# Another order of work in the mixers, the attention, the first feed-forward's head and the last norm, and thirteen products of zeros at the start

## What is computed

```python
# first block
xn = rms_norm(h, g_mix_pre); z = xn @ w_in
y_conf = conformer_conv(...)     # 31-tap depthwise convolution, layer norm, silu, 256x256 product
y_att  = forgetting_attention(...)  # 4 heads, causal, cumulated log gates in the logits
y_sc   = short_conv_mixer(...)   # 3 taps
y_pool = multiscale_pool(...)
h = h + rms_norm(concat(y_conf, y_att, y_sc, y_pool) @ w_out, g_mix_post)
h = h + rms_norm(square(relu(hn @ w_up)) @ w_down, g_mlp_post)
h = h + rms_norm((p @ w_ple_proj) * sigmoid(rms_norm(h) @ w_ple_gate), g_ple_post)
# second block, layer 0: latent attention (8 heads) and differential attention (8 maps), then swiglu
# second block, layer 1: recurrent mixer (state space heads and hgrn2), then swiglu, then the last norm
x = x + swiglu(rms_norm(x), w_gate, w_up, w_down)
out = rms_norm(x, norm_final)
```

## Time and profile before

| | us |
|---|---|
| median of 3 runs | 1001.95 (999.59 to 1003.36) |
| profiled execution | 1000.06 |
| its span, first to last instruction | 998.2 |
| mean granted TensorE clock | 0.992 of full |
| TensorE busy | 953.5 |
| VectorE, ScalarE, GpSimd busy | 700.3, 515.8, 87.1 |
| moved by transfers | 164.4 MB, 165 GB/s on average |

### The profile page before, as it was taken

The page is one execution under the profiler, slowest core; times in us unless marked ns, Lnnn a source line. Parts: engine busy times, 40 slices in busy tenths (PEclk is TensorE's granted clock), DMA queues, the critical chain, the costliest instruction groups (busy, mean ns, idle before and its releaser), DMA issues.

```text
span 998.2 us, 13575 instructions
## 1 busy us (share of the span) xinstructions
PE 953.5 (96%) x5540; PEld 835.9 (84%) x5540; DVE 700.3 (70%) x921; ACT 515.8 (52%) x698; POOL 87.1 (9%) x110
## 2 busy tenths in 40 slices
PE   6997999999999899889999999999989889999997
PEld 5996797888888688778988888888988789888886
DVE  4798785666667887886666666667979676666663
ACT  4776754444436646765543434368645355434341
POOL 4353000000000100000000000000132000000000
PEclk9999999999999999989999999999999999999999
DMA  9732365665565354224665656546321356656531
GB/s 320 245 128 92 120 220 194 199 207 183 174 206 175 112 171 143 85 85 125 215 208 173 207 171 209 169 149 211 127 85 49 121 169 211 207 172 208 172 127 43
DMA packets 106190, 164.40 MB, mean 165 GB/s; under 512 B 2816, under 2 KB 82784, under 8 KB 106000
## 3 DMA queue, kind: packets, MB, share of 16 engines
q1 hardware_dynamic: 104688, 158.25, 48.9%
q0 software_dynamic: 1440, 5.28, 1.5%
HBM read 162.47 MB, written 1.05 MB: 164 GB/s over the span
## 4 chain that ended last, share of the span: by engine, by line
PE 69%; DVE 19%; ACT 6%; issue 4%; DMA 2%; POOL 1%; DVEq 0%; POOLq 0%; ACTq 0%
PE ps L379 67%; DVE wl L1739 6%; DVE SC L1841 2%; PE ps L387 2%; ACT wh L1172 2%; DMA raw<-in_w_in 1%; DVE xhl L1744 1%; DVE xf L1748 1%; ACT junk L1160 1%; DVE st L2139 1%; ACT xhl L1178 1%; POOL st L2496 1%; DVE rows L2339 1%; DVE hs L1759 0%; DVE h L1801 0%
## 5 line engine op out<-in xcount | busy, mean ns | idle before, releaser
L1739 DVE TENSOR_TENSOR wl<-raw,wh 128x2048 fp32r<-128x2048 f32 (+2 forms) x150 | 339.6, 2266 | 153.8 <-ACT wh L1172 153.6
L1172 ACT ACTIVATE wh<-raw 128x2048 fp32r<-128x2048 f32 (+2 forms) x150 | 281.9, 1884 | 156.6 <-PE ps L379 142.8
L379 PE MATMUL ps<-xhl,wh 128*128 128x512 f32 (+1 forms) x1248 | 257.9, 354 | 2.5 <-ACT wh L1237 2.5
L379 PEld LDWEIGHTS ps<-xhl,wh 128*128 128x128 f32 x1248 | 202.4, 193 | 29.9 <-issue 3.7
L379 PE MATMUL ps<-wh,xhl 128*128 128x512 f32 (+3 forms) x1000 | 195.2, 339 | 6.0 <-ACT SC L1435 1.8
L379 PEld LDWEIGHTS ps<-wh,xhl 128*128 128x128 f32 x1000 | 155.1, 190 | 25.3 <-ACT xhl L1178 2.6
L379 PEld LDWEIGHTS ps<-xhl,wl 128*128 128x128 f32 x1008 | 135.6, 191 | 7.5
L379 PE MATMUL ps<-xhl,wl 128*128 128x256 f32 x1008 | 140.6, 282 | 0.0
L379 PE MATMUL ps<-wl,xhl 128*128 128x512 f32 (+3 forms) x500 | 105.2, 336 | 0.0
L379 PE MATMUL ps<-wh,fh 128*128 128x512 f32 x304 | 91.0, 392 | 1.8 <-DVE fl L1986 1.5
L379 PE MATMUL ps<-wh,fl 128*128 128x512 f32 x304 | 90.2, 390 | 0.0
(11 more groups left out here) (266 smaller groups left out, 840.8 us busy)
## 6 DMA issues: line engine op xcount, KB each, us to landing
raw<-in_ffn_gate SPq DMA_DIRECT2D x22, 1024.0 KB, 5.3
raw<-in_ffn_up SPq DMA_DIRECT2D x22, 1024.0 KB, 5.4
raw<-in_ffn_down SPq DMA_DIRECT2D x22, 1024.0 KB, 4.9
raw<-in_w_up SPq DMA_DIRECT2D x16, 1024.0 KB, 5.6
raw<-in_w_down SPq DMA_DIRECT2D x16, 1024.0 KB, 4.9
raw<-in_s_w_in SPq DMA_DIRECT2D x14, 1024.0 KB, 5.4
raw<-in_w_in SPq DMA_DIRECT2D x9, 1024.0 KB, 7.1
raw<-in_a_w_in SPq DMA_DIRECT2D x6, 1024.0 KB, 5.1
```

The costliest lines, as they stand in the source:

```text
L379: return e.matmul(o, a, b, start=start, stop=stop, skip_group_check=True)
L1172: e.activation(high_of(i), raw_of(i), ACT.Copy).then_inc(*up("act_high", i))
L1739: e.tensor_tensor(low_of(i), raw_of(i), high_of(i).bitcast(F32), ALU.subtract).then_inc(*up("dve_lo", i))
```

## The change

It reorders steps on all engines, adds 13 products of zeros into an unused result bank at TensorE's start (`warm`), moves four copies (xs, cb) from ScalarE to VectorE and splits the last norm's product between VectorE and ScalarE. No weight slot is added or left out. The diff is cut to the changed lines, each group with the line before it, and indentation is reduced.

```diff
@@ -479,7 +479,7 @@
-def project_end(n, sl, tb, half, order):
+def project_end(n, sl, tb, half, order, x_low=None):
@@ -487,6 +487,8 @@
         for x in (xh, xl):
+            if x is xl and i == order[2] and x_low:
+                e.wait_ge(*x_low)
@@ -513,9 +515,18 @@
 def first_mixer():
+    def warm(n):
+        for i in range(n):
+            mm(ps[7][:, 0:256], upad[:, 0, 0:128], upad[:, 0, 0:256], True, True)
+    e.wait_ge(*at("pool_zero", 2))
+    warm(6)
...
     norm_turn(0, 0)
+    warm(2)
     norm_turn(0, 1)
+    warm(5)
@@ -670,9 +681,9 @@
-    def down_block(j, tb):
+    def down_block(j, tb, halves=(0, 1)):
         x = [y[:, j % 3, :].rearrange("p (k n) -> p k n", k=2) for y in (fh, fl)]
-        tok(down[j], [(ps[ACC[s_next][tb][c]][:, :], HALF[c]) for c in range(2)], tb, 0, j == 0, False, x)
+        tok(down[j], [(ps[ACC[s_next][tb][c]][:, :], HALF[c]) for c in halves], tb, 0, j == 0, False, x)
@@ -725,14 +736,16 @@
         e.wait_ge(*at("dve_head_low", l, 0, 4))
-        down_block(0, 0)
+        down_block(0, 0, (0,))
+        e.wait_ge(*at("dve_head", l, 1, 0))
+        head_turn(1, 0, 4, 7)
+        down_block(0, 0, (1,))
         e.wait_ge(*at("dve_head", l, 1, 1))
-        head_turn(1, 0, 4, 7)
         head_turn(1, 4, 2, 2)
-        e.wait_ge(*at("dve_head_low", l, 1, 4))
-        down_block(0, 1)
...
         head_turn(1, 6, 2, 5)
+        e.wait_ge(*at("dve_head_low", l, 1, 0))
+        down_block(0, 1)
@@ -828,6 +841,8 @@
         if i == 8:
+            e.wait_ge(*at("act_qk_turned", 1, 1, 0))
+        if i == 9:
@@ -894,7 +909,7 @@
         if i == 1:
-            e.wait_ge(*at("act_qk_turned", 1, 0, 0))
+            e.wait_ge(*at("act_qk_turned", 0, 0, 1))
@@ -1010,7 +1025,7 @@
             elif n == 1:
-                e.wait_ge(*at("act_cb", tb))
+                e.wait_ge(*at("dve_cb", tb))
@@ -1025,7 +1040,7 @@
         if n == 0:
-            e.wait_ge(*at("act_xs", 0))
+            e.wait_ge(*at("dve_xs", 0))
@@ -1087,7 +1102,6 @@
     e.wait_ge(*at("act_xbc", 3))
-    feat(S["hq"][1], ps[0])
@@ -1098,6 +1112,7 @@
         mm(o[:, 256:384], xb[:, 4 + g, 128:256], xb[:, 6 + g, 128:256], True, True).then_inc(*up("pe_cb", g))
+    feat(S["hq"][1], ps[0])
@@ -1128,9 +1143,9 @@
     project(6, sl, 0, 1, order, at("dve_mix3_low", 0, 1))
-    e.wait_ge(*at("dve_mix3_low", 1, 0))
+    e.wait_ge(*at("act_part_high", 6, 1, 0))
     for half in range(2):
-        project_end(6, sl, 0, half, order)
+        project_end(6, sl, 0, half, order, at("dve_mix3_low", 1, 0))
@@ -1309,22 +1324,22 @@
     forget_exp(1)
-    highs(10)
+    taps(22, 24)
...
     forget_probs(1)
-    taps(22, 26)
+    highs(10)
+    taps(24, 27)
...
             *up("act_pool_out", t))
-    taps(26, 29)
+    taps(27, TAPS)
...
             *up("act_short_tap", t))
-    taps(29, TAPS)
@@ -1338,9 +1353,9 @@
     forget_out(1)
-    forget_probs(3)
...
     e.activation(sg[:, 0:256], ps[1][:, 0:256], ACT.Sqrt, bias=P("eps")).then_inc(*up("act_conf_std"))
+    forget_probs(3)
@@ -1558,7 +1573,8 @@
                              ACT.Copy).then_inc(*up("act_qk_turned", j, tb, c))
-    tick(7, do)
+        if c == 0:
+            tick(7, do)
@@ -1644,7 +1660,7 @@
     conv_silu(3)
-    for i in range(2):
+    def queries(i):
@@ -1662,16 +1678,12 @@
+    queries(0)
     decay(0)
-    for tb in range(2):
-        e.wait_ge(*at("pe_xs", tb))
-        e.activation(xs[:, tb, :], ps[(7, 1)[tb]][:, :], ACT.Copy).then_inc(*up("act_xs", tb))
     decay(1)
-    for g in range(2):
-        e.wait_ge(*at("pe_cb", g))
-        e.activation(cbs[:, g, :], ps[(2, 5)[g]][:, 0:384], ACT.Copy).then_inc(*up("act_cb", g))
...
     seg(0)
+    queries(1)
@@ -1705,11 +1717,13 @@
     highs(S["sout"][3])
-    for tb in range(2):
-        e.wait_ge(*at("dve_mix3_x", 1, tb))
-        part_high(4, 8, tb, (6, 1, tb))
+    e.wait_ge(*at("dve_mix3_x", 1, 0))
+    part_high(4, 8, 0, (6, 1, 0))
+    highs(UP["f1"][0][0])
+    e.wait_ge(*at("dve_mix3_x", 1, 1))
+    part_high(4, 8, 1, (6, 1, 1))
     norm_squares(6, 0)
-    highs(UP["f1"][0][0])
+    highs(UP["f1"][0][1])
@@ -1723,8 +1737,12 @@
 ffn("f1")
-norm_squares(7, 0)
-norm_squares(7, 1)
+for tb in range(2):
+    norm_squares(7, tb)
+    e.wait_ge(*at("pool_rstd", "norm", 7, tb))
+    e.wait_ge(*at("dve_final", tb, 1))
+    e.activation(hs[:, tb, HALF[1]], hs[:, tb, HALF[1]], ACT.Identity, scale=st[:, 3 * tb + 2:3 * tb + 3]).then_inc(
+        *up("act_out", tb))
@@ -1907,24 +1925,22 @@
     lows(7)
-    taps(11, 17)
-    lows(8)
-    taps(17, 20)
+    taps(11, 16)
...
     forget_bias(3)
-    lows(9)
-    taps(20, 23)
+    lows(8)
...
     forget_inverse(1)
+    taps(16, 19)
+    lows(9)
...
                     hsb.rearrange("p (t n) -> p t n", t=2), ALU.mult).then_inc(*up("dve_short_in"))
-    taps(23, 25)
+    taps(19, 21)
     forget_max(2)
-    lows(10)
-    taps(25, TAPS)
+    taps(21, TAPS)
@@ -1935,16 +1951,17 @@
         *up("dve_short_out"))
-    mix_low(3)
...
     e.tensor_tensor(csq, cacc, cacc, ALU.mult).then_inc(*up("dve_conf_square"))
+    mix_low(3)
     forget_max(3)
+    lows(10)
     mix_low(2)
+    forget_inverse(3)
     lows(11)
-    forget_inverse(3)
@@ -2009,13 +2026,14 @@
         head_turned(0, 4, 2, 2)
+        lows(ups[3][0] + 2)
+        head_block(1)
         lows(ups[3][0] + 3)
-        head_block(1)
...
         head_turned(1, 4, 2, 2)
-        lows(down[0] + 3)
...
         head_turned(1, 6, 2, 5)
+        lows(down[0] + 3)
@@ -2223,7 +2241,7 @@
         tick(t, do)
-        if t == 8:
+        if t == 10:
@@ -2323,6 +2341,13 @@
     conv(3)
+    lows(S["xbc"][2] + 4)
+    for tb in range(2):
+        e.wait_ge(*at("pe_xs", tb))
+        e.tensor_copy(xs[:, tb, :], ps[(7, 1)[tb]][:, :]).then_inc(*up("dve_xs", tb))
+    for g in range(2):
+        e.wait_ge(*at("pe_cb", g))
+        e.tensor_copy(cbs[:, g, :], ps[(2, 5)[g]][:, 0:384]).then_inc(*up("dve_cb", g))
@@ -2412,18 +2437,21 @@
         gained(4, 4, tb, (3, 4)[tb], P("g_norm").to_broadcast([128, 4])).then_inc(*up("dve_mix3_x", 1, tb))
+    def gated_columns_low(tb):
...
+    e.wait_ge(*at("dve_cb", 1))
+    e.wait_ge(*at("dve_dt_turned"))
+    decayed(0)
...
     weigh(1)
+    decayed(1)
...
     score(8)
-    e.wait_ge(*at("act_cb", 1))
-    decayed(0)
-    decayed(1)
@@ -2444,28 +2472,30 @@
     state_out(1)
-    lows(S["sout"][2])
...
     gated_mean(0)
+    gated_mean(1)
     state_columns(1)
-    gated_mean(1)
+    gated_out(0)
     state_low(1)
-    for tb in range(2):
-        gated_out(tb)
+    gated_out(1)
+    gated_columns(0)
+    lows(S["sout"][2])
+    gated_columns_low(0)
     lows(S["sout"][3])
-    for tb in range(2):
-        gated_columns(tb)
+    lows(UP["f1"][0][0])
+    gated_columns(1)
+    gated_columns_low(1)
...
     norm_rows(6, 0)
-    lows(UP["f1"][0][0])
     norm_low(6, 0)
+    residual(6, 1)
     lows(UP["f1"][0][1])
-    residual(6, 1)
+    norm_mean(6, 1)
     lows(UP["f1"][1][0])
-    norm_mean(6, 1)
+    norm_scale(6, 1)
     lows(UP["f1"][1][1])
-    norm_scale(6, 1)
@@ -2482,10 +2512,12 @@
     e.wait_ge(*at("dma_row1", 1))
+    for c in (1, 0):
+        e.tensor_tensor(hs[:, tb, HALF[c]], h[:, tb, HALF[c]], rows[:, 1, HALF[c]], ALU.mult).then_inc(
+            *up("dve_final", tb, c))
     e.wait_ge(*at("pool_rstd", "norm", 7, tb))
-    for c in range(2):
-        e.scalar_tensor_tensor(hs[:, tb, HALF[c]], h[:, tb, HALF[c]], r, rows[:, 1, HALF[c]], ALU.mult,
-                               ALU.mult).then_inc(*up("dve_out", tb, c))
+    e.wait_ge(*at("dve_final", tb, 0))
+    e.tensor_scalar(hs[:, tb, HALF[0]], hs[:, tb, HALF[0]], r, None, ALU.mult).then_inc(*up("dve_out", tb))
@@ -2564,7 +2596,7 @@
     if n >= 2:
-        e.wait_ge(*at("dve_weighed", n - 2))
+        e.wait_ge(*at("dve_weighed", max(1, n - 2)))
@@ -2598,7 +2630,7 @@
     for c in range(2):
-        e.wait_ge(*at("dve_out", tb, c))
+        e.wait_ge(*(at("act_out", tb) if c else at("dve_out", tb)))
...
```

## The result

The changed kernel took **986.87 us** in the median of 4 runs (986.59 to 988.45), the kernel before 1000.97 us in the same comparison (4 runs, 999.59 to 1003.36); ratio 0.986, 95% interval 0.9836 to 0.9884. The profiled execution took 986.59 us with a span of 984.8, 13.4 less than before's 998.2, and my sum had been 10.1.

A forecast was written before the change was run, and what follows sets the result against it. TensorE was taken as the bound, busy 953.5 of 998.2 us, so only idle time can be won. Terms 0.2 + 2.7 + 0.8 + 0.8 + 1.5 + 4.1 + 0 = 10.1 gave 990.0, against the median 991.8; range 987 to 996.5.

The forecast's parts named there:

- First mixer: Mean product 3.5 us earlier through earlier last taps, then 1.3 given back, 0.8 for the root; 2.7 us taken, bounds 1.0 and 4.5.
- Thirteen products: At TensorE's start, products of zeros raise its rate, but the mixer hangs on transfers and taps: 0.2 us taken.
- First feed-forward: Wait of 1.53 us for block 1's low parts shortened, last turns done earlier: 0.8 us taken, bounds 0 and 1.5.
- Attention: mix(5) 2.9 us earlier, map 10's maximum only 0.9, new wait near 427: 0.8 us taken, bounds -1 and 3.
- Recurrent mixer, first part: Work moved ahead of the last query projection, copies to VectorE: 1.5 us taken, bounds 0.3 and 2.5.
- End: Recurrent mixer's end: four waits of 5.1 us go, new ones of 0.65 and 0.35 come; 4.1 us taken.
- Last norm: First half ready 0.4 us later, second 0.7 earlier, last transfer starts as before: 0 taken, bounds -0.3 and +0.4.
- (a): Rival: ScalarE's table loads run only after their waits, recurrent start gains 0.3 us, total 993; chance 0.12.
- (b): Rival: VectorE stays the bound in the mixers; mixer 1.0, attention 0, end 3, total 5.8, so 996.1 us; chance 0.15.
- (c): Rival: TensorE's start is on the path after all, 2.1 us more, 989.7; chance 0.04.
- (d): Rival: products of zeros don't raise the rate and delay the second transposes, -1.8 for 0.2, 993.8 us; chance 0.06.
- (e): Rival: TensorE's clock falls in attention and stays at half, costing up to 19 us, total 1011; chance 0.03.

The follow-up runs named there:

- run 1: Changed kernel without the thirteen products of zeros and their wait at TensorE's start: 987.39 us.
- run 6: Changed kernel with the low part of weight slot 10 back ahead of VectorE's last ten taps: 989.64 us.
- run 4: Changed kernel with ScalarE's taps, probabilities and split back in the old order, VectorE's new order kept: 987.14 us.
- run 5: Changed kernel with head 3's probabilities back ahead of the square root on ScalarE: 987.01 us.
- run 9: Changed kernel with six float32 products of constants in TensorE's wait before the mean product: 986.34 us.
- run 2: Kernel before with only the first mixer's new order on ScalarE and VectorE: 995.32 us against 1000.25.
- run 10: Changed kernel with the attention's low part at tick 7, split at tick 10, constant products before the mean product, mix(5) and map 9's turn: 983.25 us.
- run 11: The kernel of run 10 with seven more constant products, before the attention's first projection and second transposes: 982.96 us.
- 12: Kernel before with only the recurrent mixer's changes, both parts: 993.23 us against 1001.65.

## Why the prediction was right or wrong

**What bounds the kernel: right but for the attention.** By run 1 nearly all of the gain is TensorE's idle time. In the attention and f0 it is not: there idle time went from 9.10 to 9.32 us, and busy time from 302.20 to 300.74, as the clock was at 0.50 for 6.8 us in place of 10.2 (two falls of 3.4 and 6.8 us before, one of 6.8 after). That the change can win only idle time did not hold there.

**First mixer: right that the last taps bound it, too small by 2.3 us.** This is the term that took the total out of the range. Three steps of it failed.
- "GpSimd's seven last taps at 1.1 us then end near 82", "last tap near 84.9". The last tap ended at 83.61. From 86.05, less the low part of 2.2 us, my 84.9 lets the thirty taps get 1.05 us dearer, for more of them beside GpSimd; they got 0.26 cheaper (21.14 to 20.88 us), with as many beside GpSimd as before. So the 4.8 us at the mean product are 2.3 for GpSimd, which no longer ends last, and 2.4 for VectorE, of which the low part is 2.2; run 6 puts it back and gets 2.23. GpSimd's additions took 1.00 us and ended at 80.73, 1.3 us ahead of my 82, but run 4 shows that this moves nothing. I had also put ScalarE's order first; run 4 gives it nothing.
- Two of TensorE's waits between the mean and the pointwise product were not in my list of nine stretches. I counted only the first mixer's 3.06 us, and these 1.43 us went as well, and neither run 4 nor run 5 brings them back. The 0.31 stand in the earlier trace rows; the larger one, from TensorE's timeline of the kernel before:

```profile
100.83 0.94 PE L379 MATMUL ps<-fs,SC 128*128 128x128 f32 x6 [1.12 <-ACT fs L1294]
```

- The term gave back 1.3 us for the short convolution and took 0.5 for the root. Measured, TensorE loses 1.1 us between the two products by working at half clock, of which run 9 shows 0.4 to be real. The root's new place is worth 0.1 to 0.3 us (run 5), not 0.8.

In sum: 4.8 by the mean product, 1.4 for the two waits, less 1.0 for the rest.

**Thirteen products: right.** 0.4 us by run 1, 0.05 by run 2's mean product, against 0.2. The first six ended at 6.6, before the transposes (at the prediction's 0.91 us each from 2 us on they would have ended at 7.5, 0.1 to 0.2 too late and not half a microsecond). The reason given, that the mixer hangs on transfers and taps and not on TensorE, holds for the taps; the lead went into waits for VectorE.

**First feed-forward: right.** The wait of 1.53 us became 0.69; the stretch gained 0.8.

**Attention: right within what can be told.** The 1.2 us of the table are one pair of runs; the mean of the runs with the new code is 0.6 us below that of the runs with the old. Mix(5) came 3.9 us earlier, not 2.9, map 10's maximum 1.7, not 0.9. The new wait near 427 is there (at 423.80) and so is the fall behind it.

**Recurrent mixer, first part: right,** 1.5 for 1.5, twice. The load of 1.28 us at 720.50 ran inside ScalarE's wait. **End: 5.0 for 4.1.** The four waits went, and the two that I had put in their place with 0.65 and 0.35 us were 0.36 and 0.09; TensorE's idle time in the stretch fell by 4.6 us (5.23 to 0.61), its busy time by the other 0.4 (62.03 to 61.67), for which I have no cause.

**Last norm: 0.4 us lost where I had taken 0** and no more than 0.3 as the bound. The forecast had the first half ready 0.4 us later and the second transfer issued as before, and both came so; that the end stays where it was did not follow. The rows, before and after (SPq: SyncE issues two transfers):

```profile
993.72 0.55 POOL L2496 TENSOR_TENSOR st<-st,prm 128x1 f32<-128x1 f32 x1 [7.61 <-DVE st L2482]
...
995.15 0.99 SPq L2602 DMA_DIRECT2D out<-hs  x2
```

```profile
979.92 0.93 POOL L2528 TENSOR_TENSOR st<-st,prm 128x1 f32<-128x1 f32 x1 [7.23 <-DVE st L2512]
...
979.76 1.28 DVE L2516 TENSOR_TENSOR hs<-h,rows 128x512 f32<-128x512 f32 x2
...
981.15 0.49 DVE L2520 TENSOR_SCALAR hs<-hs,st 128x512 f32<-128x512 f32 x1
...
981.66 0.81 SPq L2634 DMA_DIRECT2D out<-hs  x2
```

Counted from the last residual (991.95 and 978.15) the first transfer is issued at 3.51 in place of 3.20 us, the second at 3.89 in place of 3.86. The packets of the two run without a gap, from 4.03 to 5.54 us before and from 4.34 to 5.86 after: both ends moved with the first transfer, whose half is VectorE's. Its scaling stands behind VectorE's own two products, which end at 981.04. The power took 0.93 in place of 0.55 us, again beside a VectorE instruction with two inputs in SBUF; but it ended at 980.85, ahead of the products, so its length was not what held the first transfer.

**The rivals.** (a) fell: two loads ran ahead of their waits. The Trainium skill (ScalarE: Activation LUTs, What ACT_TABLE_LOAD costs) also adds a drain of 1380 ns to the load; the load at 720.50 began 0.02 us after the activation before it ended, and behind the load of 1.28 us at 724.98 the activation began at 726.27, so this trace shows no drain. (b) fell in its prices, though VectorE does stay the bound up to the mean product; its total was also added wrongly, as its terms (1.0, 0 and 3, the others as forecast) give 6.5 us and not 5.8, so 995.5. (c) fell by run 1. (d): the split after the second transposes started 0.7 us earlier, not later. (e): the clock fell from 422.2 to 429.0, and the fall of the earlier trace rows lasted as long, 6.8 us (425.2 to 432.0).

**The range.** The miss of 4.9 us is the 3.3 of the sum and 1.6 of the base: I had added the 1.9 us by which before's median lay above its profiled run, and the changed kernel's lies 0.3 above. The first mixer's bound was 4.5 and it gave 5.2; without the two small waits, which no bound held, it would have given 3.8.

Left open: which of VectorE's other moves in the first mixer (the maxima of heads 0 and 1, those of head 3, the order of the halves' low parts) carries the rest beside the 2.6 us of slot 10, GpSimd's earlier end above all; none was tried alone. Open too is why the start differs between kernels with the same start, by up to 0.5 us at 59; starts of single instructions of two runs should not be read finer than that.

## What to carry to other kernels

When a long chain of small steps on VectorE runs beside GpSimd, ask which of the two ends last, and price the chain as a whole: here thirty taps took 20.9 to 21.1 us in three orders, and more only when GpSimd had more to do. A block of 2.2 us ahead of the chain moved its end by 2.2. List every wait of the engine that bounds, also the small ones after the stretch you look at; 1.4 of the 5.2 us lay there. Products of constants in the waits kept TensorE's clock up here, but such a product is worth only what of the slow stretch covers no other wait: measure the second wait before counting the first.

## What was not expected of the hardware

- GpSimd made one addition of 128x256 in 0.85 to 1.0 us beside VectorE's taps, and one took 2.60 us beside a subtraction of 128x2048 that had begun 0.29 us ahead of it (run 6): it was held until the other ended, while VectorE's 2.28 us did not grow (2.29). The other way round VectorE pays: in the changed kernel a subtraction that began 0.15 us behind an addition took 2.83 us:

```profile
66.87 0.83 POOL L2559 TENSOR_TENSOR SC<-SC,fs 128x256 f32<-128x256 f32 x1
...
67.02 2.83 DVE L1757 TENSOR_TENSOR wl<-raw,wh 128x2048 fp32r<-128x2048 f32 x1
```

- The granted clock falls at different places in kernels that are the same there. The changed kernel shows 1.00 from 340 to 350, run 10 shows 0.83, with the same wait of 2.2 us before (2.21 and 2.25 us); in run 11, with that wait filled, it is 1.00 again. Five of the twelve experiments show a fall between 330 and 350, the changed kernel none. With one and the same code for the attention, the stretch from its first projection to f0's end took 309.73 to 310.59 us in seven kernels and 310.33 to 311.30 in three others, so a difference of under 1 us in a single profile's span should not be read.
- At the start the profile's granted clock reads 1.00 while the same 32 products take 6.45 us without and 4.07 us with the thirteen ahead of them. The row of the clock does not show that slower rate; only the durations do. In runs 2 and 12, which have the start of before, the row does read 0.50, from 14.5 to 17.9, and there the same products take 5.55 and 5.54 us, less than in the runs whose row reads 1.00.
